# All 64 gate batches beside the last 64 u blocks, with the first-key columns shared 1 : 1 : 2 between VectorE, ScalarE and GpSimd

## What is computed

```python
def peer_ffn(h, wq, subkeys, u, v):
    q = (h @ wq).reshape(B, S, PEER_HEADS, 2, PEER_QDIM // 2)
    sub_scores = jnp.einsum('bshpk,hpnk->bshpn', q, subkeys)
    top_v, top_i = lax.top_k(sub_scores, PEER_TOPK)
    cand = (top_v[..., 0, :, None] + top_v[..., 1, None, :]).reshape(B, S, PEER_HEADS, PEER_TOPK * PEER_TOPK)
    cand_i = (top_i[..., 0, :, None] * N_KEYS + top_i[..., 1, None, :]).reshape(...)
    best_v, best_pos = lax.top_k(cand, PEER_TOPK)
    expert = jnp.take_along_axis(cand_i, best_pos, axis=-1)
    gates = jax.nn.softmax(best_v, axis=-1)
    ...
        ub = jnp.take(u, eb, axis=0)
        hid = jax.nn.gelu(jnp.einsum('tkd,td->tk', ub, xb), approximate=False) * gb
        vb = jnp.take(v, eb, axis=0)
        return jnp.einsum('tk,tkd->td', hid, vb)
```

## Time and profile before

| | us |
|---|---|
| median of 3 runs | 2865.7 |
| lowest, highest | 2865.52, 2867.83 |
| span of the profiled execution | 2863.0 |
| TensorE busy | 2716.7 (95%) |
| VectorE busy | 1595.0 (56%) |
| ScalarE busy | 937.4 (33%) |
| GpSimd busy | 1362.7 (48%) |

### The profile page before, as it was taken

How to read it: one execution, slowest core, us unless ns; L and a number is a source line. 1 busy time by engine, 2 the same in 40 slices (tenths; PEclk the granted TensorE clock), 3 DMA queues, 4 the chain that set the end, 5 groups by cost and what they waited for, 6 DMA issues and landing times.

```text
span 2863.0 us, 32244 instructions
## 1 busy us (share of the span) xinstructions
PE 2716.7 (95%) x12062; PEld 2057.0 (72%) x12062; DVE 1595.0 (56%) x3064; ACT 937.4 (33%) x1684; POOL 1362.7 (48%) x1004
## 2 busy tenths in 40 slices
PE   8989999998999899999998789999999999999996
PEld 7856888776888678888777678888888864444442
DVE  1033044476314343440224757999999999756667
ACT  3275343655424333222334433111113670000001
POOL 4432444566446234444352436645446664645445
PEclk9999999999999999999999899999999999999999
DMA  5321233332244136663331035999999849999998
GB/s 164 104 58 30 74 105 92 113 102 70 102 141 145 53 93 194 206 185 123 78 105 38 30 110 205 377 409 408 409 409 385 318 146 409 409 411 409 410 409 327
DMA packets 219373, 598.85 MB, mean 209 GB/s; under 512 B 22337, under 2 KB 47314, under 8 KB 218834
## 3 DMA queue, kind: packets, MB, share of 16 engines
q1 hardware_dynamic: 135280, 300.70, 30.7%
q0 software_dynamic: 75968, 275.81, 24.9%
q10 hardware_dynamic: 7970, 20.28, 2.2%
HBM read 584.84 MB, written 7.41 MB: 207 GB/s over the span
## 4 chain that ended last, share of the span: by engine, by line
PE 72%; DMA 11%; DVE 9%; POOL 3%; ACT 2%; issue 2%; POOLq 0%; DVEq 0%; ACTq 0%; SPq 0%
PE ps L1893 14%; PE ps L1373 14%; PE ps L1374 13%; PE ps L1375 13%; DMA rows<-in_v,expert 6%; DMA rows<-in_u,expert 5%; DVE ps L2597 2%; PE ps L1882 2%; DVE rows L2583 2%; PE ps L1339 1%; POOL wlo L1148 1%; PE ps L1912 1%; PE ps L1472 1%; POOL rows L1279 1%; PE ps L1559 1%
## 5 line engine op out<-in xcount | busy, mean ns | idle before, releaser
L1148 POOL TENSOR_TENSOR wlo<-wraw,whi 128x1024 fp32r<-128x1024 f32 x258 | 627.3, 2442 | 799.5 <-ACT whi L614 709.8
L614 ACT ACTIVATE whi<-wraw 128x1024 fp32r<-128x1024 f32 x258 | 270.0, 1058 | 693.0 <-PE ps L1375 593.4
L1928 PE MATMUL ps<-stream,hg 128*128 128x512 f32 x1024 | 441.7, 594 | 7.8 <-DMA stream<-in_v 7.0
L1893 PE MATMUL ps<-haff,stream 128*128 128x256 f32 x2048 | 445.6, 379 | 2.2 <-ACT stg L1038 2.2
L1373 PE MATMUL ps<-hhi,whi 128*128 128x512 f32 x1088 | 428.4, 394 | 15.6 <-DVE hlo L2059 8.7
L1893 PEld LDWEIGHTS ps<-haff,stream 128*128 128x128 f32 x2048 | 388.0, 190 | 53.8 <-ACT stg L1038 2.4
L1375 PE MATMUL ps<-hhi,wlo 128*128 128x512 f32 x1088 | 425.5, 391 | 0.0
L1374 PE MATMUL ps<-hlo,whi 128*128 128x512 f32 x1088 | 425.3, 391 | 0.0
L1279 POOL DMA_INDIRECT rows<-in_u,expert x256 | 275.6, 1077 | 239.8 <-DVE hid L2583 122.4
L1928 PEld LDWEIGHTS ps<-stream,hg 128*128 128x128 f32 x1024 | 195.2, 191 | 253.6 <-issue 244.8
L2583 DVE CUSTOM_DVE_ANT_0 rows<-rows,h_s 128x1024 f32<-128x1024 f32 x256 | 318.4, 1247 | 83.4 <-DMA rows<-in_u,expert 83.2
(11 more groups left out here) (485 smaller groups left out, 4331.8 us busy)
## 6 DMA issues: line engine op xcount, KB each, us to landing
stream<-in_ut SPq DMA_DIRECT2D x128, 512.0 KB, 6.8
stream<-in_v SPq DMA_DIRECT2D x128, 512.0 KB, 6.8
wraw<-in_w_in SPq DMA_DIRECT2D x96, 512.0 KB, 3.6
wraw<-in_w_ada SPq DMA_DIRECT2D x48, 512.0 KB, 4.1
wraw<-in_w_gu SPq DMA_DIRECT2D x88, 256.0 KB, 3.7
wraw<-in_w_down SPq DMA_DIRECT2D x22, 512.0 KB, 3.5
decs<-acs_kept ACTq DMA_DIRECT2D x16, 512.0 KB, 3.6
wraw<-in_w_br_ssm SPq DMA_DIRECT2D x16, 512.0 KB, 3.5
```

Source lines behind the costliest of these rows:

```text
L614: act.activation(whi[:, n % WSLOTS, 0:kn, :], wraw[:, n % WSLOTS, 0:kn, :], ACT.Copy).then_inc(w_hi, 1)
L1148: pool.tensor_tensor(wlo[:, n % WSLOTS, 0:kn, :], wraw[:, n % WSLOTS, 0:kn, :], whi[:, n % WSLOTS, 0:kn, :].bitcast(F32), ALU.subtract).th ...
L1893: ins = pe.matmul(ps[:, n % 2, 0:ND], stream[j][:, k, :], haff2[:, 1, k, :], start=k == 0, stop=k == KD - 1)
L1928: ins = pe.matmul(ps[:, 2 * i + half, :], hg[:, n, P * i:P * i + P], stream[j][:, 4 * half:4 * half + 4, :], start=n == 0, stop=n == NKEYS ...
```

## The change

Seven things change.

1. `AHEAD` becomes 64 (ND // 4), so `AHEAD_FROM` is 65: a gate batch stands behind each of the u blocks 64 to 127, none is left for later, and `PE_HOLE`, `gate_matrices` and `hole_diagonal` go. The 16 rows of PE_HOLE are VectorE's.
2. The heads of tiles 2 and 3 are made before the blocks begin, directly behind those of tile 0. `WOVEN` says in which of the eight places a row goes: four for tile 0, three for tiles 2 and 3, all for tile 1, whose heads stand in blocks 15 to 18.
3. VectorE's batch b stands behind row 98 + 9 b // 4, so 2, 2, 2 and 3 rows apart; `scale_gates` behind row 82.
4. The second-key half is made by ScalarE: relu(1 - (iota - key)^2), four squares and one relu over 512 columns, from `slot_k`. Of the first-key columns VectorE makes token 0's, ScalarE token 1's, GpSimd those of tokens 2 and 3 (two of the four `hot_pool` buffers for each batch).
5. `mix(b)` no longer multiplies ones that a memset wrote: for blocks still to come it copies the gates into hg, for the others it multiplies. It waits for the gelu of block 64 + b. `late_mix` takes as many tokens as have their gates.
6. `GELU_AT` puts five of eight row_gelu behind u blocks 66 and later, where two were behind blocks with a batch.
7. Score loads (`load_scores`) stand at the rows of `LOADS`; those for tile 1 wait for u block 127.

```diff
-AHEAD = 20
+WOVEN = {0: (1, 3, 5, 7), 2: (1, 4, 7), 3: (1, 4, 7), 1: range(8)}
+AHEAD = ND // 4
-AHEAD_ROW = 199
-HOT_DVE, HOT_ACT, HOT_POOL = (0,), (1, 2), (3,)
-GELU_AT = {4: 0, 21: 1, 30: 2, 49: 3, 69: 4, 88: 5, 110: 6, 117: 7}
+AHEAD_ROW = 98
+HOT_DVE, HOT_ACT, HOT_POOL = (0,), (1,), (2, 3)
+GELU_AT = {4: 0, 17: 1, 50: 2, 66: 3, 81: 4, 95: 5, 109: 6, 116: 7}
+GATES_AT = AHEAD_ROW - 16
+LOADS = {26: (0, 1), **{28 + 6 * q: (q,) for q in range(2, 8)}, 248: (8, 9), 266: (10,), 282: (11,)}
...
+def batch_row(b):
+    return AHEAD_ROW + 9 * b // 4
...
-                mine = hot1_of(b)
+                first, second = hot1_of(b), hot2_of(b)
+                for m in range(4):
+                    c = 4 * b + m
+                    act.activation(second[:, m, :], cst[:, C_IOTA:C_IOTA + P], ACT.Square, bias=slot_k[:, c:c + 1])
...
                 link(ins)
+                act.activation(second.rearrange("p m n -> p (m n)"), second.rearrange("p m n -> p (m n)"), ACT.Relu, bias=1.0, scale=-1.0)
...
-                if n == 98:
+                if n == AHEAD_FROM - 5:
                     act.wait_ge(s("head_done"), top_done(3, PEER_HEADS - 1))
...
-            for b in range(AHEAD, ND // 4):
-                hots(b)
-                if b == AHEAD:
-                    row_diags(PE_HOLE[:DIAGS])
...
+                if q >= 8:
+                    pool.wait_ge(s("u_mm"), NKEYS)
...
-                if b >= POOL_HOTS:
-                    pool.wait_ge(s("mix_mm"), b - POOL_HOTS + 1)
+                if b >= 2:
+                    pool.wait_ge(s("mix_mm"), b - 1)
...
+            hot_before = {batch_row(b) + RING - 4: b for b in range(AHEAD)}
...
-                    pe.wait_ge(s("late_mixed"), n - AHEAD_FROM)
+                    pe.wait_ge(s("late_mixed"), n - AHEAD_FROM - 1)
...
-                    between()
+                    if places[0] in WOVEN[t]:
+                        between()
+                    places[0] += 1
...
-                v.tensor_tensor(hot2_of(b), cst[:, C_IOTA:C_IOTA + P].unsqueeze(1).to_broadcast([P, 4, P]),
-                                ps[:, 3, 4 * b:4 * b + 4].unsqueeze(2).to_broadcast([P, 4, P]), ALU.is_equal)
...
+                now = AHEAD_FROM + b
+                v.wait_ge(s("hg_ready"), now)
                 v.wait_ge(s("mix_mm"), b + 1)
...
+                if now < NKEYS:
+                    v.tensor_copy(hg[:, now:NKEYS, 4 * b:4 * b + 4], gates[:, now:NKEYS, :])
+                view = hg[:, 0:now, 4 * b:4 * b + 4]
+                v.tensor_tensor(view, view, gates[:, 0:now, :], ALU.mult).then_inc(s("mixed"), 1)
...
+            for t, h in TOP_ORDER[PEER_HEADS:3 * PEER_HEADS]:
+                top_keys(t, h, between=next_row)
             for b, (kind, t, h) in enumerate(BLOCKS):
```

More of the change, by code:

```diff
@@ L91, with late_tokens @@
 ENDS = (0, 2, 3, 1)
-NA = 4 * AHEAD
-HOLE_HALF = {AHEAD + 3 + 5 * x // 4: x for x in range(2 * TOPK)}
-HOLE_DIAG = {AHEAD + 4 + 5 * (2 * r + 1) // 4: r + DIAGS for r in range(TOPK - DIAGS)}
-HOLE_NEXT = [AHEAD + 7 + 5 * (2 * r + 1) // 4 for r in range(14)]
+def batch_row(b):
+    return AHEAD_ROW + 9 * b // 4
+def late_tokens(n):
+    return 4 * (n - AHEAD_FROM + 1)
 C_IDENT, C_NEGGE, C_NEGONE, C_LE, C_GT, C_ONE = (P * i for i in range(6))
@@ L1116, in scalar_program @@
                     hots(n - AHEAD_FROM + 2)
-            for b in range(AHEAD, ND // 4):
-                hots(b)
-                if b == AHEAD:
-                    row_diags(PE_HOLE[:DIAGS])
-            for h in range(len(GELU_AT), PEER_HEADS):
-                row_gelu(0, h)
             for h in range(PEER_HEADS):
@@ L1880, in gate_batch @@
                 for m in range(4):
-                    first = hot_pool[:, b % POOL_HOTS, :] if m in HOT_POOL else hot1_of(b)[:, m, :]
+                    first = hot_pool[:, pool_slot(b, m), :] if m in HOT_POOL else hot1_of(b)[:, m, :]
                     ins = pe.matmul(ps[:, gate_bank(b), P * m:P * m + P], hot2_of(b)[:, m, :], first, start=True, stop=True)
@@ L1930, in tensor_program @@
                 ins.then_inc(s("v_mm"), 1)
-            for r in range(len(PE_HOLE), len(PE_ROWS)):
+            for r in range(len(PE_ROWS)):
                 ins = row_half(r, 0)
@@ L2696, in later_weights @@
                 head_weights(*BLOCKS[b][1:]).then_inc(s("wrow_ready"), 1)
-            def gate_matrices():
-                later_weights(PE_HOLE[-1][0])
-                v.wait_ge(s("hg_ready"), NKEYS)
-                hots(AHEAD)
-                for m in range(AHEAD, ND // 4):
-                    if m + 1 < ND // 4:
-                        hots(m + 1)
-                    mix(m)
-                    if m in HOLE_DIAG:
-                        hole_diagonal(HOLE_DIAG[m])
-                v.wait_ge(s("pe_row_used"), TOPK)
-            between_rows = {**{divmod(AHEAD_ROW + 2 * b, TOPK): partial(batch_ahead, b) for b in range(AHEAD)}, divmod(AHEAD_ROW - 2, TOPK): first_ahead,
+            between_rows = {**{divmod(batch_row(b), TOPK): partial(batch_ahead, b) for b in range(AHEAD)}, divmod(GATES_AT, TOPK): scale_gates, divmod(AHEAD_ROW - 2, TOPK): first_ahead,
                             (26, 15): lambda: later_weights(29), (27, 15): lambda: later_weights(30),
```

108 lines of the change are left out of this document (33 added, 75 removed).

## The result

The changed kernel takes **2922.4 us** (median of 4 runs, 2918.7 to 2928.5) where the kernel before, run beside it, takes 2866.3 (2865.5 to 2867.8): a ratio of 1.0198, 95% interval 1.0183 to 1.0212. It is 56 us slower; the prediction was 2921. The span of its profiled execution is 2919.3 us, and that of the kernel before 2863.0. Which parts of the prediction carried this, and which were right by luck, is the subject of the rest.

What follows compares the result with a forecast made beforehand. It took transfers at 409 GB/s, and the units left when v blocks begin, as the bound. Span 2863.0 + 35.5 (later v blocks) + 20 (units left) = 2918.5, so time 2921 us; range from below 2878 to above 2948.

Steps and rivals of the forecast that it cites:

- What bounds: Last 1050 us: transfers at 409 GB/s limit; units left when the v blocks begin, and when that is, count.
- Tops first: Heads of tiles 2 and 3 before the batches: rows fall behind, transfers idle a quarter, first gate batch at 2058.
- TensorE's two waits ahead of it: Before the first batch: TensorE idle about 10 us behind u block 62, and again behind block 64.
- Cadence: The 64 gate batches, one per u block: 323 us from first batch towards the v blocks, which start at 2385.
- Beside u rows: 28 batches where VectorE's u rows stop GpSimd's pair of columns: 6.0 us each, 168 us.
- Row_gelu: Two table loads behind five batch blocks: TensorE waits 2.0 us each time, where it was 0.86 twice.
- Beside v rows: 35 batches: GpSimd at 4.40 us each or TensorE with gelu stalls, whichever is slower per run; 159 us.
- What is left: From the v blocks on: 249 gathers out instead of 261, 15.5 units at 1.282 us, 20 us.
- The late score load: Tile 1's score load waits for u block 127, holding gathers from row 248: nothing, up to 10 us.
- GpSimd fits: Rival: hot columns slip between u rows, TensorE sets the pace; v blocks at 2346, time 2882; chance 0.22.
- Held longer: Rival: GpSimd takes 6.5 us beside u rows (+14), late gathers starve VectorE beside v rows (+10); 2945 us; chance 0.18.
- the other side: Rival: first batch at 2037, no GpSimd limit, v blocks at 2323; 2859 us, or 2849 with gelu stalls hidden; chance 0.03.

Runs made afterwards that it cites:

- gates_early: The changed kernel with the Exp of heads 2 to 7 of tile 0 taken together behind u block 17, so later row_gelu load no table: 2925.9 us.
- both: The changed kernel with one first-key column on GpSimd, two on VectorE, and the Exp of tile 0's heads 2 to 7 behind u block 17: 2877.2 us.
- extra_loads: The changed kernel with twelve more 512 KB transfers from SyncE beside the v blocks, into unused memory: 2941.3 us.
- dve_two: The changed kernel with one first-key column on GpSimd (token 3) and two on VectorE (tokens 0 and 2): 2890.8 us.
- sooner_only: The changed kernel with only the batches placed earlier (first behind row 84 instead of 98, 22/9 rows apart, scale_gates and row_gelu moved to suit): 2938.7 us.
- sooner: On top of both: first batch behind row 84 instead of 98, batches 22/9 rows apart, scale_gates and row_gelu moved to suit: 2877.7 us.

## Why the prediction came out

Point by point, in its own order:

- **What bounds.** Right. Beside v blocks the kernel after moves 409 GB/s (2640 to 2840), and in all runs with 247 to 249 gathers out the end comes 536 to 544 us behind the start of the v blocks, whatever was done before (without the run that adds transfers). So "how many units are left when the v blocks begin, and when that is" holds in 11 kernels.
- **Tops first.** Right to 2 us: heads of tile 0 at 1843.8 predicted and 1843.2 measured, of tile 3 at 2021.6 and 2019.8; 305 GB/s for "near 300"; first batch 2058 and 2059.4. TensorE's two waits ahead of it, "about 10 us" and another, are 4.8 and 14.3.
- **Cadence.** The sum was right (323 us predicted for 63 intervals, 321.3 measured), its parts were not. *Beside u rows* I took 6.0 for each of 28 batches. Measured are runs such as 5.32, 6.23, 7.42, 6.19, 4.42: a pair of columns caught by u rows gives mostly 5.3 to 7.5, one that is not keeps 4.35. All intervals together are 47 us over 63 x 4.35, of which 17 stand at row_gelu and 2 at the first, so 28 are GpSimd's: 5.35 for a u batch, where I had 42 in all. *Row_gelu* I priced at its wait, 2.0 us, five times, of which some 7 us stand in the sum of 323. It costs 17.2, since in four of five cases the interval behind it is long too. TensorE's timeline of the kernel after shows how:

```profile
2076.53 0.70 PE L1871 MATMUL ps<-hot_ahead 128*128 128x128 f32 x4 [1.88 <-issue]
2077.05 1.04 PE L1871 MATMUL ps<-hot_pool,hot_ahead 128*128 128x128 f32 x4
2077.88 4.91 PE L1882 MATMUL ps<-haff,stream 128*128 128x256 f32 x16
```

  The u block behind the wait takes 4.91 us for its 16 instructions where others take 3.62, and the granted clock from 2078 to 2082 is 0.69: part of it at the lower level, 1.2 instead of 2.4 GHz. I had charged this for the long idle spell only. The misses, 14 too much for GpSimd and 10 too little for row_gelu, cancelled but for the 2 at the first interval; that the sum came out is luck. *Beside v rows* batches are 4.35 apart, so TensorE set the pace there and not GpSimd with 4.40.
- **The terms were not a sum.** The prediction added GpSimd's excess and row_gelu's stalls. The runs price the first at 32 us when taken away alone, the second at nothing (gates_early), and the second at 11 once the first is gone (both). The total was right because both were counted as they lie in one timeline; as prices of repairs they would have misled.
- **What is left.** 20 us predicted, 22.8 measured; the start of the v blocks 2385 and 2383.0, gathers out 249 and 248. The count was near: 15.5 units predicted, and when the v blocks end, 49 rows are left instead of 31, 18 more. The mis-sized term is the price of one: 1.282 us as a transfer, but 1.39 where it is paid, behind the v blocks, because VectorE sums every row there until TensorE's share begins (extra_loads). 18 x 1.39 = 25 us, and that part is longer by 23. The late score load, at "nothing, or up to 10 us", made VectorE wait 6.6 us once; as the transfers still run at 402 GB/s from 2385 to 2600, little of it can have been lost.
- **The rivals.** "GpSimd fits" gave 2882 and v blocks at 2346; dve_two is that case, with 2890.8 and 2351.4. "Held longer" (2945) is nearly the time of sooner_only (2938.7), by the first half of its reason, longer waits for GpSimd; VectorE waits for no row beside its batches. For the other side, a first batch at 2037 and no limit by GpSimd were to give v blocks at 2323 and 2859 us, or 2849 without row_gelu's stalls. sooner has the start (2037.4), no row_gelu stalls, and 10 us of waits for GpSimd instead of the changed kernel's 33.5 (before the first batch included), and gets 2336.7 and 2877.7. What that rival left out is VectorE's own total, 468.8 of the 495.4 us: it let TensorE's chain run free, and didn't ask who uses the 240 rows.

Against the kernel before the balance is then: beside the heads of tiles 2 and 3 the changed order moves 305 of 409 GB/s for 176 us, some 45 us of transfers lost. What it removes, the late stretch (2275 to 2349 at 121 GB/s in the kernel before), was 52. With both repairs the v blocks do begin 8.3 us earlier than before, but with 13 gathers fewer out, and these cost 25 (by the profiled executions; they lie 17 us apart, the medians 11). The idle transfers were moved, not removed.
